# Making half of a cross-attention memory's keys first in a one-core hybrid trunk kernel

## The reference

```python
def rms_norm(x, g):
    y = x * lax.rsqrt(jnp.mean(x * x, axis=-1, keepdims=True) + EPS)
    return y * g

xn = rms_norm(h, norm_mix)
proj = xn @ w_in            # forgetting attention, mLSTM and gates
...
h = h + merged @ w_mix_out
hn, memn = rms_norm(h, norm_xattn), rms_norm(mem, norm_mem)
q = hn @ wq
k, v = split(memn @ wkv)    # 256 x 1024 each, 4 heads of 256
h = h + softmax(q k^T / 16) v @ wo
h = h + relu(rms_norm(h, norm_mlp) @ w_mlp_in) ** 2 @ w_mlp_out
return rms_norm(h, norm_final)
```

## Time and profile before

| | before |
|---|---|
| three runs | 950.94, 950.98 and 952.46 us, median 950.98 us |
| the profiled execution | 950.93 us, its span 949.2 us |
| matrix engine busy | 934.5 us (98% of the span), 4653 matmuls |
| VectorE, ScalarE, GpSimd busy | 552.1, 408.9, 14.3 us |
| transfers | 92.62 MB, mean 98 GB/s |

### The profile page before, as it was taken

One profiled execution on the slowest core, in us unless ns is written; L12 is line 12 of the kernel. 1 busy time (PEld: TensorE's weight loads), 2 busy tenths in 40 slices (PEclk: granted clock), 3 DMA queues, 4 the chain that ended last, 5 costly groups with the idle time before them and its releaser, 6 DMA issues.

```text
span 949.2 us, 11881 instructions
## 1 busy us (share of the span) xinstructions
PE 934.5 (98%) x4653; PEld 761.5 (80%) x4653; DVE 552.1 (58%) x979; ACT 408.9 (43%) x676; POOL 14.3 (2%) x38
## 2 busy tenths in 40 slices
PE   7999999999999999999999999999999999999997
PEld 6878777777777878889988678998888888888885
DVE  6632676342556763777334534768847866885544
ACT  4431556344424333344434433366446445634522
POOL 4000000000000000000000000000000000000000
PEclk9999999999999999999999999999999999999999
DMA  9311221122111272333521242120441261062202
GB/s 287 126 40 61 90 89 45 46 89 89 47 43 45 89 266 82 118 135 105 184 89 45 92 174 87 47 90 0 153 158 45 89 223 45 0 218 93 89 1 88
DMA packets 44815, 92.62 MB, mean 98 GB/s; under 512 B 1772, under 2 KB 1864, under 8 KB 44760
## 3 DMA queue, kind: packets, MB, share of 16 engines
q1 hardware_dynamic: 43192, 86.54, 27.1%
q0 software_dynamic: 1568, 5.32, 1.7%
HBM read 89.76 MB, written 2.10 MB: 97 GB/s over the span
## 4 chain that ended last, share of the span: by engine, by line
PE 92%; DVE 4%; ACT 2%; DMA 1%; issue 1%; SPq 0%; ACTq 0%; DVEq 0%
PE bank L1351 68%; PE bank L1382 12%; DVE w_lo L988 2%; PE bank L1555 1%; PE bank L1449 1%; PE bank L1476 1%; PE bank L1461 1%; PE bank L1395 1%; PE bank L1506 1%; PE bank L1493 1%; ACT w_hi L737 1%; PE bank L1533 1%; PE bank L1520 1%; DMA stage<-in_w_in 1%; PE bank L1494 0%
## 5 line engine op out<-in xcount | busy, mean ns | idle before, releaser
L988 DVE TENSOR_TENSOR w_lo<-stage,w_hi 128x1024 fp32r<-128x1024 f32 x174 | 205.1, 1221 | 89.5 <-ACT w_hi L737 89.2
L1351 PE MATMUL bank<-act_hi,w_hi 128*128 128x512 f32 (+1 forms) x640 | 247.8, 387 | 0.1
L1351 PE MATMUL bank<-act_hi,w_lo 128*128 128x512 f32 (+1 forms) x640 | 242.7, 379 | 0.0
L1351 PE MATMUL bank<-act_lo,w_hi 128*128 128x512 f32 (+1 forms) x640 | 242.4, 379 | 0.0
L737 ACT ACTIVATE w_hi<-stage 128x1024 fp32r<-128x1024 f32 x174 | 174.3, 1051 | 98.6 <-PE bank L1351 36.5
L1351 PEld LDWEIGHTS bank<-act_hi,w_lo 128*128 128x128 f32 x640 | 120.3, 188 | 23.1
L1351 PEld LDWEIGHTS bank<-act_hi,w_hi 128*128 128x128 f32 x640 | 120.6, 188 | 21.9 <-DVE w_lo L988 0.6
L1351 PEld LDWEIGHTS bank<-act_lo,w_hi 128*128 128x128 f32 x640 | 120.6, 188 | 21.4
L1351 PE MATMUL bank<-w_hi,act_hi 128*128 128x512 f32 x256 | 101.6, 397 | 4.0 <-DVE act_lo L1176 2.6
L1351 PE MATMUL bank<-w_hi,act_lo 128*128 128x512 f32 x256 | 99.8, 390 | 0.0
L1351 PE MATMUL bank<-w_lo,act_hi 128*128 128x512 f32 x256 | 99.7, 389 | 0.0
(11 more groups left out here) (260 smaller groups left out, 1266.0 us busy)
## 6 DMA issues: line engine op xcount, KB each, us to landing
stage<-in_w_in SPq DMA_DIRECT2D x20, 1024.0 KB, 4.9
stage<-in_w_mlp_in SPq DMA_DIRECT2D x16, 1024.0 KB, 5.2
stage<-in_w_mlp_out SPq DMA_DIRECT2D x16, 1024.0 KB, 5.6
stage<-in_w_xkv SPq DMA_DIRECT2D x8, 1024.0 KB, 4.9
stage<-in_w_mix_out SPq DMA_DIRECT2D x4, 1024.0 KB, 5.0
stage<-in_w_xq SPq DMA_DIRECT2D x4, 1024.0 KB, 5.3
stage<-in_w_xo SPq DMA_DIRECT2D x4, 1024.0 KB, 5.0
x_tok<-in_x SPq DMA_DIRECT2D x4, 512.0 KB, 10.0
```

What stands on the lines that cost most here:

```text
L988: dve.tensor_tensor(w_lo[:, r:r + 2, :], stage_pair(pair), w_hi[:, r:r + 2, :].bitcast(F32), ALU.subtract).then_inc(s_low, 1)
L1351: ins = pe.matmul(dst, still[q], moving[q], start=(k == 0 and q == 0), stop=(k == nk - 1 and q == 2))
```

## The change

The unit `mem_k0` moves from behind `mix1` to the very front. The memory and its weights are loaded first, each in pieces; x, its gains (`row_a`) and the small weights of POOL follow behind them. The first keys are made without the inverse root of the norm: the raw memory is transposed, multiplied by its gains (now one number for each partition, `mem_gain`, from a transpose of `gain_rows`) and split, and the products go slab by slab over all four groups into two PSUM banks (`mem_products`). The root of both memory tiles (`mem_root`) is found later, turned into a row for all partitions by a product of ones with a diagonal matrix (`mem_factors`), and multiplied into the finished keys (`mem_keys`). As the places of `mem_hi`, `mem_lo` and the first keys are needed by others in between, POOL writes these 2.5 MB to DRAM (`kept_hi`, `kept_lo`, `kept_k`) and loads them back when `merge_split` is over (`s_back`). `mem_k1` then is alone between `mix1` and `x_q0`; its scaling by `mem_factor` is on DVE, and the values' scaling by the root is in ACT's copy. The warm-up has 6 products in place of 20, and the turns of token tiles 2 and 3 in `fox_v` stand at the ends of groups 1 and 2.

The diff, cut to its core (lines left out are marked; the left out parts rename indices and add semaphores):

```diff
@@ -35,7 +35,7 @@
-WARM_UP = 20
+WARM_UP = 6
@@ -54,6 +54,7 @@
+        ("mem_k0", "w_xkv", 0, KT, 0, 4),
@@ -71,7 +72,6 @@
-        ("mem_k0", "w_xkv", 0, KT, 0, 4),
@@ -97,7 +97,7 @@
-GROUP0 = [sum(u[5] for u in UNITS[:n] if u[3] <= KT) for n in range(len(UNITS) + 1)]
+GROUP0 = [sum(u[5] for u in UNITS[1:n] if u[3] <= KT) for n in range(len(UNITS) + 1)]
@@ -117,6 +117,9 @@
+            continue
+        if n == 0:
+            halves += [(n, j, c, 0, MEM) for c in cs for j in groups]
@@ -218,11 +221,20 @@
-    steps += [("norm", 0), ("split_weights", 0), ("norm_turn", 0), ("norm_split", 0), ("split_weights", 1),
-              ("norm", 1), ("split_weights", 2), ("norm_root", 1), ("split_weights", 3), ("norm_scale", 1)]
-    after(1, ("norm_turn", 1), ("norm_split", 1), ("norm", 2))
-    after(2, ("norm_turn", 2), ("norm_split", 2), ("norm", 3))
-    after(4, ("norm_turn", 3), ("norm_split", 3), ("split_weights", 4), ("split_weights", 5))
+    steps += [("mem_gains", 0), ("mem_turn", 0), ("mem_split", 0), ("split_weights", 0), ("mem_split", 1),
+              ("mem_turn", 1), ("mem_split", 2), ("mem_split", 3)]
+    after(0, ("split_weights", 1), ("mem_turn", 2), ("mem_split", 4), ("mem_split", 5))
+    after(1, ("split_weights", 2), ("mem_turn", 3), ("mem_split", 6), ("mem_split", 7))
+    after(2, ("split_weights", 3), ("norm", 0))
+    before(3, ("mem_squares", 0), ("mem_squares", 1))
+    after(3, ("split_weights", 4))
+    before(7, ("norm_turn", 0), ("norm_split", 0), ("split_weights", 5), ("norm", 1))
+    after(7, ("norm_root", 1), ("norm_scale", 1))
+    after(first("fox_v"), ("mem_root", 0))
+    after(first("fox_v") + 1, ("norm_turn", 1), ("norm_split", 1), ("norm", 2))
+    after(first("fox_v") + 2, ("mem_factors", 0), ("mem_keys", 0))
+    after(first("fox_v") + 3, ("norm_turn", 2), ("norm_split", 2), ("norm", 3))
+    after(first("fox_v") + 5, ("norm_turn", 3), ("norm_split", 3))
@@ -278,12 +290,7 @@
-    h = first("mix0")
-    for i in range(MEM // P):
-        after(h + 2 * i + 2, ("norm", NT + i))
-        after(h + 2 * i + 4, ("norm_turn", NT + i), ("norm_split", NT + i))
...
-    for unit, n0, last in (("mix1", NT + 2, 5), ("x_out1", 2 * NT + 2, 6)):
+    for unit, n0, last in (("mix1", NT, 5), ("x_out1", 2 * NT, 6)):
@@ -313,7 +320,8 @@
-    quiet = {"up_fox0": first("gate_fox1") + 4, "gate_ml1": first("up_ml0") - 1, "mlp_in1": first("mlp_in0") + 5}
+    quiet = {"up_fox0": first("gate_fox1") + 4, "gate_ml1": first("up_ml0") - 1, "mlp_in1": first("mlp_in0") + 5,
+             "x_q0": first("mem_k1") + 3}
@@ -322,7 +330,7 @@
-        pairs.setdefault(max(at_half, quiet.get(UNITS[n][0], 0)), []).append(pair)
+        pairs.setdefault(max(at_half, FIRST_HALF[1] - 1, quiet.get(UNITS[n][0], 0)), []).append(pair)
@@ -459,7 +467,11 @@
-        x_tok = at("x_tok", 24, [P, NT, DM])
...
+        mem_tok, mem_square = at("mem_tok", 0, [P, MEM // P, DM]), at("mem_square", 16, [P, MEM // P, DM])
+        mem_diag = at("mem_diag", 85, [P, MEM // P, P])
+        mem_factor = at("mem_factor", 128, [P, MEM])
+        x_tok = at("x_tok", 40, [P, NT, DM])
@@ -469,7 +481,6 @@
-        mem_tok = at("mem_tok", 86.5, [P, MEM // P, DM])
@@ -482,6 +493,10 @@
+        kept_hi = nc.dram_tensor("kept_hi", (P, KT, MEM), F32).ap()
+        kept_lo = nc.dram_tensor("kept_lo", (P, KT, MEM), F32).ap()
+        kept_k = nc.dram_tensor("kept_k", (P, 4, MEM), F32).ap()
@@ -616,8 +633,13 @@
-            load_x(0)
-            sp.dma_start(row_a[:], norm_mix.partition_broadcast(P)).then_inc(s_row_x, 16)
+            def load_mem(c):
+                cols = slice(HALF_W * c, HALF_W * (c + 1))
+                sp.dma_start(mem_tok[:, :, cols], mem.rearrange("(i p) n -> p i n", p=P)[:, :, cols])\
+                  .then_inc(s_mem[c], 16)
...
+            load_mem(0)
+            sp.dma_start(gain_rows[:], norm_mem.rearrange("(k p) -> k p", p=P)).then_inc(s_gains, 16)
@@ -631,14 +653,22 @@
-                if lot < 2:
+                if lot == 0:
+                    sp.dma_start(stage[buf][:, 0:1, :], src[:, 0:1, :]).then_inc(s_slab, 16)
+                    sp.dma_start(stage[buf][:, 1:2, :], src[:, 1:2, :]).then_inc(s_first[0], 16)
+                    load_mem(1)
+                    sp.dma_start(stage[buf][:, 2:4, :], src[:, 2:4, :]).then_inc(s_lot[buf], 16)
+                elif lot == 1:
...
+                    load_x(0)
...
-                if lot == 0:
+                if lot == 1:
+                    sp.dma_start(row_a[:], norm_mix.partition_broadcast(P)).then_inc(s_row_x, 16)
+                if lot == 2:
...
-                if lot == 1:
+                if lot == 3:
@@ -703,6 +735,7 @@
+            pool.wait_ge(s_xt[NT - 1], 16)
@@ -711,23 +744,30 @@
+            pool.wait_ge(s_memhigh, KT)
+            pool.wait_ge(s_low, 8)
+            pool.dma_start(kept_hi, mem_hi[:].bitcast(F32)).then_inc(s_kept, 16)
+            pool.wait_ge(s_memlow, KT)
+            pool.dma_start(kept_lo, mem_lo[:].bitcast(F32)).then_inc(s_kept, 16)
+            pool.wait_ge(s_memkeys, 4)
+            pool.dma_start(kept_k, mem_k[:, 0:4, :]).then_inc(s_kept, 16)
+            pool.wait_ge(s_kept, 16 * 3)
+            pool.memset(conv_u[:, :, 0:CONV_K - 1], 0.0).then_inc(s_pad, 1)
...
-            pool.wait_ge(s_yml, ML_HEADS)
-            pool.dma_start(mem_tok[:], mem.rearrange("(i p) n -> p i n", p=P)).then_inc(s_mem, 16)
-            pool.wait_ge(s_merl, KT)
...
+            pool.wait_ge(s_merl, KT)
...
+            pool.dma_start(mem_hi[:].bitcast(F32), kept_hi).then_inc(s_back, 16)
+            pool.dma_start(mem_lo[:].bitcast(F32), kept_lo).then_inc(s_back, 16)
+            pool.dma_start(mem_k[:, 0:4, :], kept_k).then_inc(s_back, 16)
...
-            pool.wait_ge(s_scaled, 2 * (2 * NT + 2))
+            pool.wait_ge(s_scaled, 2 * 2 * NT)
@@ -739,8 +779,14 @@
-                elif pair in (0, 2):
-                    act.wait_ge(s_first[pair // 2], 16)
+                elif pair == 0:
+                    act.wait_ge(s_slab, 16)
+                    copy(w_hi[:, 0:1, :], stage_pair(0)[:, 0:1, :]).then_inc(s_slabhigh, 1)
+                    act.wait_ge(s_first[0], 16)
+                    copy(w_hi[:, 1:2, :], stage_pair(0)[:, 1:2, :]).then_inc(s_high, 1)
+                    return
+                elif pair == 2:
+                    act.wait_ge(s_first[1], 16)
@@ -788,12 +834,11 @@
-                elif k == "mem_k":
-                    copy(mem_k[:, 4 * order(n) + j, :], b[:, 0:MEM]).then_inc(free, 1)
...
-                    copy(mem_v[:, j, HALF_W * order(n):HALF_W * (order(n) + 1)], b[:]).then_inc(free, 1)
+                    copy(mem_v[:, j, HALF_W * order(n):HALF_W * (order(n) + 1)], b[:], scale=mem_stat[:, 2, j:j + 1])\
+                        .then_inc(free, 1)
@@ -859,6 +902,22 @@
+                elif step == "mem_gains":
+                    act.wait_ge(s_gainturn, 1)
+                    copy(mem_gain[:], bank[1][:, 0:KT]).then_inc(s_gain, 1)
+                elif step == "mem_split":
+                    act.wait_ge(s_memturn, n // 2 + 1)
+                    if n == 0:
+                        act.wait_ge(s_gain, 1)
+                    copy(mem_hi[:, n, :], mem_turned(n), scale=mem_gain[:, n:n + 1]).then_inc(s_memhigh, 1)
+                elif step == "mem_squares":
+                    for s in s_mem:
+                        act.wait_ge(s, 16)
+                    act.activation(mem_square[:, n, :], mem_tok[:, n, :], ACT.Square, accum_out=mem_stat[:, 0, n:n + 1])\
+                        .then_inc(s_memsquares, 1)
+                elif step == "mem_factors":
+                    act.wait_ge(s_memrows, 1)
+                    copy(mem_factor[:], bank[5][:, 0:MEM]).then_inc(s_memfactor, 1)
@@ -1092,6 +1162,9 @@
+                elif k == "mem_k":
+                    group_done(dve, g)
+                    dve.tensor_tensor(mem_k[:, 4 + j, :], b[:, 0:MEM], mem_factor[:], ALU.mult).then_inc(free, 1)
@@ -1168,6 +1241,22 @@
+                elif step == "mem_split":
+                    dve.wait_ge(s_memhigh, n + 1)
+                    dve.scalar_tensor_tensor(mem_lo[:, n, :], mem_turned(n), mem_gain[:, n:n + 1],
+                                             mem_hi[:, n, :].bitcast(F32), ALU.mult, ALU.subtract).then_inc(s_memlow, 1)
+                elif step == "mem_root":
+                    dve.wait_ge(s_memsquares, MEM // P)
+                    half_mean_square(mem_stat[:, 1, :], mem_stat[:, 0, :], DM)
+                    inverse_root(mem_stat[:, 2, :], mem_stat[:, 1, :], mem_stat[:, 3, :])
+                    for i in range(MEM // P):
+                        dve.tensor_scalar(mem_diag[:, i, :], ident[:], mem_stat[:, 2, i:i + 1], None, ALU.mult)\
+                           .then_inc(s_memdiag, 1)
+                elif step == "mem_keys":
+                    dve.wait_ge(s_half, KT)
+                    dve.wait_ge(s_memfactor, 1)
+                    for j in range(4):
```

(34 more changed lines are left out.)

120 lines of the change are left out of this document (74 added, 46 removed).

## The result

The changed kernel takes 960.12 us (median of 4 runs, 958.65 to 960.71), beside 951.72 us for the kernel before in the same comparison (950.94 to 952.48): ratio 1.008, 95% interval 1.0068 to 1.0092. It is slower, as forecast, but by more than twice the amount, and beyond the range. The profiled execution took 960.34 us, 958.3 of it span.

What follows compares the result with a forecast made beforehand. The matrix engine, busy for 98% of the span, was taken as the bound: 950.93 + 15.4 (later `fox_q`) + 1.4 (clock) - 13.3 (middle) + 0.2 (key bank) = 954.6 us, range 951.0 to 958.5.

Steps and rivals of the forecast that it cites:

- first product of keys: At the very start: the first key product starts at 6.9 us, with the memory's first half landing at 4.1.
- from there to the turn of tile 0, with the clock's 1.4: At the start: seven slabs of 12 key products, 10.1 us, two turns and short waits, plus 1.4 for a slow clock.
- turn of tile 0 to the start of group 1: In `fox_v`: the turn begins at 18.0 us, and group 1 starts at 33.9 after DVE's queue.
- the wait in it: Ahead of `fox_v`'s group 1: the matrix engine waits 5.0 us for DVE's `act_lo`, behind memory's root and `fox_q` pairs.
- start of group 1 to `fox_q`: In `fox_v`: groups 1 to 3 take 16.4 us, the row of factors 0.35, two turns 4.4.
- a turn at a group's end: Turns of tiles 2 and 3 in `fox_v`: each shows 2.2 us of turn, ACT, DVE and hops.
- `fox_q`: Its first product marks the start's end: 55.1 us before the clock's term, 15.4 later than the 39.7 before.
- given back in the middle, less the key bank: Between `mix0` and `x_q0`: 11.5 us of keys and 1.75 of turns saved, 0.2 lost to a bank freed late.
- no new wait at `x_q0`: At `x_q0`: 11.5 us of keys are left as cover, with 2 us of slack, so no wait appears.
- the clock: At the start: full clock comes at 10 us rather than about 6.5, costing 1.4 us, between none and 2.4.
- the clock falls once more: Rival: clock falls in the 5 us wait ahead of group 1, whose first half takes 5.4, not 2.7; 957.2, chance 0.20.
- The rival "faster": Rival: up to `fox_q` the matrix engine never waits for DVE, waits shrink by 5.5 us; 943.3 us, chance 0.08.

Runs made afterwards that it cites:

- the hole filled: The changed kernel with 28 unused products of ones behind the turn of token tile 1: 958.25 us (1.0065), then 957.58 (1.0057).
- root late: The changed kernel with the memory's root, diagonal tiles, factors and first key scaling moved to the end of `fox_v`: 958.70 us, 1.0058; second run 959.38.
- weights late: The changed kernel with the split of `fox_q`'s first weights moved behind the sixth half of `fox_v`: 957.14 us, 1.0046.
- the start filled: The changed kernel with 12 unused products of ones behind the memory's second turn: 959.89 us, 1.0081.
- the order alone: The changed kernel with memory's root, factors, keys and `fox_q`'s first weights later in `fox_v`, turns of tiles 2 and 3 half a group earlier: 952.2 us, 1.0000.
- The only version measured as faster: The kernel of the order alone plus 4 unused products of ones behind the memory's second turn: 950.64 us, 0.9984.

## Why the prediction was wrong

By its own steps, from the profiled executions (56.5 for `fox_q` is 55.1 and the 1.4 for the clock):

| step | predicted | measured |
|---|---|---|
| first product of keys | 6.9 | 8.27 |
| from there to the turn of tile 0, with the clock's 1.4 | 12.5 | 12.34 |
| turn of tile 0 to the start of group 1 | 15.9 | 15.74 |
| the wait in it | 5.0 | 4.93 |
| start of group 1 to `fox_q` | 21.2 | 24.05 |
| a turn at a group's end | 2.2 | 2.15 |
| `fox_q` | 56.5 | 60.40 |
| the fall at 106 us | none | 1.6 |
| given back in the middle, less the key bank | 13.1 | 13.2 |
| time | 954.6 | 960.34 |

The steps through the queues held: place, cause and length of the hole, both group ends, 11.5 us of keys and 1.75 of turns in the middle, no new wait at `x_q0`, and the size of the clock's term at the start (1.4, measured 1.3). That last one was luck. I had expected a clock that rises late, at 10 us; in this execution it had risen before 4.6 us and fell again in the wait ahead of the first key, and in the five other traces with the same beginning the term measures 1.9 to 2.8. What failed is the part on **the clock**, which assumed that once up it stays up. The case "the clock falls once more" was on the list, with the right place and price (2.7; measured 5.28 - 2.72 = 2.6, or 2.4 against the 2.84 with the hole filled), but with a chance of 0.20. The row against it was weak: it said that no hole of 5 us exists in the kernel before, which is no evidence that such a hole is harmless. (It also gave 1.23 us as the longest wait at the start, where the earlier trace rows shows 1.53 ahead of the first product.) The row for it was direct: 3.1 us after the last matmul the clock was down. The four profiles with a wait of 2.5 us or more ahead of group 1 (the change, root late, weights late, the start filled) all have the fall; the four with 0.8 us and the one with the hole filled do not. The fall ought to have been the forecast, and the sum would have been 957.2, still 3 us short.

The other 3.1 us are two smaller things. The **first product of keys** came 1.4 later. I had taken the landing of slab 0 to follow the memory at full rate; ACT waited for it until 6.77 us:

```profile
5.32 0.47 ACT L777 ACTIVATE mem_hi<-bank,mem_gain 128x256 fp32r<-128x256 f32 x1 [0.41 <-PE bank L1469]
6.77 1.28 ACT L777 ACTIVATE w_hi<-stage 128x512 fp32r<-128x512 f32 x2 [0.97 <-DMA stage<-in_w_xkv]
```

The first product started at 7.6 to 8.8 us in the other kernels with the same beginning, as ACT started on slab 0 at 6.1 to 7.3, so this term moves by more than 1 us from run to run; 6.9 was below all of them. And the **fall at 106 us** was in this profile by chance and not in that of before. The profile of before had the lowest time of its runs, 0.8 under the median of the comparison (951.72), because it had no such stretch. 954.6 + 2.6 + 1.4 + 1.6 = 960.2.

The direction was right for the reason given: what the middle gives back (13.2) is less than what the start costs, because DVE's order and not its load holds the engine. The rival "faster" needed those waits gone; with them gone by the order alone, the kernel is level (1.0000). The only version measured as faster (0.9984) has the filler at the start as well.

## What to carry to other kernels

A wait of TensorE ahead of dense work has two prices: its length, and the work behind it at half clock. Ask of each new hole whether it is long enough for the second; here 2.5 us was, though not in every execution, and 0.8 us was not. Two edits that each halve a hole may each look poor, and be worth more than their sum when made together: 6.8 us in the traces, beside 2.1 and 3.7. Where work is moved to the front, move its side work (roots, scalings, later weights) behind the next thing that the matrix engine waits for; products nobody uses can hold the clock over a wait, as those in the 4.9 us hole did, but where it is not up yet count them at half clock, or they outlast the wait.

## What the runs showed of the hardware

- The granted clock fell inside holes of 2.5, 2.7, 4.8 and 4.9 us ahead of group 1 and of 2.55 and 2.9 us at the start, 1.7 to 3.7 us after the engine had stopped, one trace each; in none of 0.8 or 1.1 us, nor in the single ones of 1.46 and 1.53 us at the start. The earlier trace rows had put the fall 3.1 us after the last matmul, so the shorter holes were a surprise. Whether the small waits just ahead (0.36 and 0.54 us in these kernels) helped the clock down wasn't tried.
- A clock of 1.2 GHz can come with an engine that the profile shows as fully busy: 106 to 110 us, right behind products of 12 columns, and the same in five more of eleven profiles. Such a stretch is 3.4 us long and costs 1.6 us. The time moves in steps, 950.9, 952.5 and 954.4; the first of these steps fits one such stretch, the second isn't explained.
- When the clock comes up at the start moves by some 3 us between executions. With the same beginning and no filler there it was up for good at 11.2 to 14.5 us in six traces; with 4 products of ones in the wait before 8.7, with 12 at about 10.4. The column of the granted clock reads 1.00 at the start even where the durations show half speed.
